# Shorter sums in the stick-breaking attention, and weighted sums two pairs behind the transposes

## The chip, the core and the metric

One NeuronCore of a Trainium2 chip runs the whole program in one launch. TensorE (PE, with its weight loads PEld), VectorE (DVE), ScalarE (ACT), GpSimd (POOL) and the DMA queue of SyncE (SP) run their own instruction lists side by side and meet only at semaphores. The metric is the device time of the launch in microseconds. Three runs of the kernel before gave 3422.81, 3422.94 and 3425.69 us; their median is 3422.94 us.

## The reference, cut to what matters

The model has two blocks on 512 tokens with 1024 features, all in float32. Two layers of the first block hold, between two feed-forward parts, a stick-breaking attention (4 heads) and a latent attention (8 heads). The second block has a sparse layer (attention over selected keys) and a dilated layer, and in each a memory attention over 256 memory tokens.

```
# stick-breaking attention, per block of 128 queries (4 heads)
z = q k^T * scale;  mask = key < query
log_not = where(mask, -softplus(z), 0)
after = reverse_cumsum(log_not, over keys) - log_not
w = where(mask, exp(log_sigmoid(z) + after), 0);  out = w v

# latent, sparse and memory attention: a softmax over keys
p = softmax(where(valid, s, NEG));  o = p v
```

The part of the change on the first attention is about `after`: for each key, the sum of `log_not` over all later keys. The part on the others is about the product `p v`.

## The kernel before, in words

Every weight is streamed in pieces of 128 x 1024 numbers. SP loads a piece, POOL splits it into a high and a low part (L524 writes the high, L526 the low part, both read and write SBUF), PE multiplies three times (high by high, low by high, high by low). Each engine's list is written by hand, in the order in which it is to run; a semaphore is waited for with `wait_ge` and raised by `then_inc`, and an instruction that waits holds all that stand behind it on its engine.

**Stick-breaking** (`stick_breaking_and_latent_heads` on PE and DVE, `stick_breaking` on ACT). The scores are kept with keys on the partitions. A unit is one block b of 128 keys of one head; a pair is the same block of two heads; `SB_PAIRS` is 2 head pairs c by 4 blocks, b = 3, 2, 1, 0. So u = 0..3 is c = 0 and u = 4..7 is c = 1. Per pair, PE writes z (L836, L838), ACT takes abs, exp and log (L1407 to L1411), DVE writes the softplus into `SBL` (L1728), PE adds the sums of the later keys into the bank of z (function `r`, L846), and ACT takes the exponential into `SBW` (L1417). In `r` the own block is multiplied by a triangle (`tri`) and every later block k by a matrix of ones (`onen`): block b = 3 takes one product, b = 0 takes four, of 512, 384, 256 and 128 columns. A float32 matmul is two records of the trace. PE runs `r` of pair u - 1 after the latent pieces and the z of pair u; `r` of the last pair stands alone at the end. DVE writes the softplus of pair u in step u, after the copies of the latent pieces.

**The other attentions** (`attend`, on PE, ACT and DVE) go over pairs of rows, a row being 128 queries of one head. In step j, PE makes the scores of pair j (L1010, L1016), transposes the probabilities of pair j - 3 (`turn_pair`, L1027), and multiplies the transposed ones of pair j - 4 by the values (`weigh`, L1045). DVE finds the row maximum of pair j (L1811) and scales the probabilities of pair j - 1 (L1820); ACT takes the exponential of pair j (L1452), then copies what PE transposed of pair j - 3 to SBUF (L1465, into `PRT`, which has 4 places for the sparse and memory attentions and 2 for the latent one), and at the end of a group of pairs the weighted sums (L1481); DVE then takes their low part (L1838). In the sparse attention DVE also runs the steps that select the keys (L1944, L1946) between the two. PE's transposes go to two banks in turn, so a group of up to 4 transposes waits until ACT has copied the group two before.

After the second memory attention DVE scales the probabilities of the dilated attention (L1894), PE transposes them (L967) and multiplies (L981). `keep_clock` (L620) issues matmuls whose results are not used.

Of the kernel before, what the change touches and what calls it, by code (L numbers as in the profile page):

```python
# [7 lines left out]
P = 128  # L8
D, S, DEPTH = 1024, 512, 2
KD = D // P  # L10
QB = S // P
# [106 lines left out]
def program(nc, A, trips):  # L118
# [3 lines left out]
    at = [-(-nc.sbuf_base // 32) * 32]  # L122
# [96 lines left out]
    def sem(name, start=0):  # L219
        credit[name] = start  # L220
        return ctx.enter_context(nc.semaphore(name))
# [22 lines left out]
    pj_done = sem("pj_done", 2)  # L244
    vt_ready, vt_done = sem("vt_ready"), sem("vt_done", 2)
    z_ready, zl_ready, zsp_ready, e_ready, w_ready = map(sem, ("z_ready", "zl_ready", "zsp_ready", "e_ready", "w_ready"))
    sbo_ready = sem("sbo_ready")
    cv_ready = sem("cv_ready")
    oh_ready, ol_ready = sem("oh_ready"), sem("ol_ready")
    ch_ready, cl_ready = sem("ch_ready"), sem("cl_ready")  # L250
# [122 lines left out]

    def ahead_of(which):

        return 2, 3

    BORDER_FILL = 3 * S
    START_FILL = {"dsa": 2 * S, "mem_dil": 2 * S}
# [206 lines left out]
    def _(pe):  # L586
# [237 lines left out]
        def stick_breaking_and_latent_heads():  # L824
# [15 lines left out]
            def r(i):  # L840
                c, b, x = SB_UNITS[i]
                pe.wait_ge(zsp_ready, n.full(zsp_ready))
                for k in range(b, QB):
                    o = sb_bank(i)[:, (k - b) * P:]
                    at = slice(sb_at(k), sb_at(k) + sb_w(k))
                    mm = pe.matmul(o, tri if k == b else onen, SBL[:, x, at], start=False, stop=k == QB - 1, skip_group_check=True)  # L846
                mm.then_inc(e_ready, 1)

            def pv(c):
# [136 lines left out]

        def attend(which, last_sums=None):
            pairs = pairs_of(which)
            ahead, late = ahead_of(which)
            pe.wait_ge(rot_done, n.now(rot_done))  # L990
            exp_base, out_base, turned_base = n.now(p_exp), n.now(ol_ready), n.now(pt_done)
            turns, weighed, group = 0, 0, 0
# [53 lines left out]
                                       skip_group_check=True)  # L1046
                mm.then_inc(pv_done, 1)

            for j in range(len(pairs) + late + 1):
                if j < len(pairs):  # L1050
                    scores(j)
                if last_sums is not None and j == 1:
                    last_sums()
                if which == "mem_dil" and j == 1:
                    dil_exchange()
                if which == "mem_dil" and j == 6:
                    pe.wait_ge(x_taken, n.full(x_taken))
                if 0 <= j - late < len(pairs):
                    turn_pair(j - late)
                if j - late - 1 >= 0:  # L1060
                    weigh(j - late - 1)
            n.full(p_exp, 2 * len(pairs))
            n.full(ol_ready, len(ends))

# [168 lines left out]
    def _(act):  # L1233
# [204 lines left out]

        def attend(which):
            pairs = pairs_of(which)  # L1440
            ahead, late = ahead_of(which)
            used_base, turns = n.now(pv_done), 0
            low_base = n.now(ol_ready)
            if which == "mla":
                n.full(ol_ready, 8)

            def exponentials(j):
                for x, row in enumerate(pairs[j]):
                    i, w = 2 * j + x, row_width(row)
                    if x == 0:  # L1450
                        act.wait_ge(nm_ready, n.full(nm_ready, 2))
                    act.activation(probs(which, i)[:, 0:w], score_bank(which, i)[:, 0:w], ACT.Exp, bias=stat[:, i % 8, 0:1],  # L1452
                                   accum_out=stat[:, i % 8, 1:2]).then_inc(p_exp, 1)

            def copy_turned(j):
                nonlocal turns
                slots = turned_slots(which)
                if j >= slots:
                    act.wait_ge(pv_done, used_base + j - slots + 1)
                if which == "mla" and j == 1:  # L1460
                    act.wait_ge(ol_ready, low_base + 4)
                for g, m in groups(pair_blocks(pairs[j])):
                    at = j % slots * 2 * S + g * P
                    act.wait_ge(pt_ready, n.full(pt_ready))
                    act.activation(PRT[which][:, at:at + m * P], PC[:, turns % 2, 0:m * P], ACT.Copy).then_inc(pt_done, 1)  # L1465
                    turns += 1

            for j in range(len(pairs) + late + 1):
                if which == "mem_dil" and j == 3:
                    dil_exchange()  # L1470
                if j < len(pairs):
                    exponentials(j)
                if which == "mla" and j == 1:
                    last_sums()
                if 0 <= j - late < len(pairs):
                    copy_turned(j - late)
                group = ended_group(which, j - late)
                if group is not None:
                    act.wait_ge(pv_done, used_base + j - late)
                    out, bank = heads_out(OH, PD[:, group % 2], which, group)  # L1480
                    act.activation(out, bank, ACT.Copy).then_inc(oh_ready, 1)  # L1481
            n.full(pv_done, len(pairs))
# [87 lines left out]
    def _(dve):  # L1570
# [152 lines left out]
        def stick_breaking_and_latent_heads():  # L1723
            def softplus(i):
                dve.wait_ge(zl_ready, n.full(zl_ready))
                if i == 2 * QB:
                    dve.wait_ge(e_ready, e_base + i)
                dve.scalar_tensor_tensor(out=SBL[:, i % 2, sb_part(i)], in0=sb_bank(i), scalar=0.0, in1=sb_exp(i),  # L1728
                                         op0=ALU.max, op1=ALU.add).then_inc(zsp_ready, 1)

            def latent_pieces(m):
                c = m // 2
                if m == 0:
                    dve.wait_ge(rc_ready, n.full(rc_ready, 2))
                dve.wait_ge(piece_used, n.full(piece_used))
                if m % 2 == 1:
                    dve.tensor_tensor(QM[:, c], PC[:, 0], RY[:], ALU.mult)
                    ins = dve.tensor_tensor(PROJ[:, c], PC[:, 1], YSS[:], ALU.mult)
                else:
                    if c < 2:  # L1740
                        dve.tensor_tensor(QM[:, 4 + c], PC[:, 1], RY[:], ALU.mult)
                    ins = dve.tensor_tensor(PROJ[:, C_SV + c], PC[:, 0], YSS[:], ALU.mult)
                ins.then_inc(mla_done, 1)
                n.full(mla_done)

            e_base = n.now(e_ready)
            for u in range(len(SB_PAIRS)):
                if u < 2:
                    softplus(2 * u)
                latent_pieces(u)  # L1750
                if u >= 2:
                    softplus(2 * u)
                softplus(2 * u + 1)
                if u in (0, 2):
                    turn([(QM[:, 4 + u // 2], P, tabM, C_PMLA)], PD[:, 1])
            n.full(e_ready, len(SB_UNITS))
# [45 lines left out]
        def attend(which, steps=None):  # L1802

            pairs = pairs_of(which)
            ahead, late = ahead_of(which)

            def peak(j):
                at = 2 * j % 8
# [10 lines left out]
                    p = probs(which, 2 * j + x)[:, 0:row_width(row)]  # L1819
                    dve.tensor_scalar(p, p, stat[:, at + x, 2:3], None, ALU.mult).then_inc(p_norm, 1)  # L1820

            for j in range(len(pairs) + late + 1):
                if which == "mem_dil" and j in (1, 2, 4):
                    (dil_spread, dil_gather, dil_factors)[(1, 2, 4).index(j)]()
                if j < len(pairs):
# [4 lines left out]
                    normalize(j - 1)  # L1830
                if which == "mla" and j in (1, 2):
                    last_sums(j)
                group = ended_group(which, j - late)
                if group is not None:
                    dve.wait_ge(oh_ready, n.full(oh_ready))
                    low, bank = heads_out(OL, PD[:, group % 2], which, group)
# [430 lines left out]
```

## Time and profile before

| what | value |
|---|---|
| median of 3 runs | 3422.94 us |
| profiled execution | 3417.32 us, span 3416.0 us |
| PE busy | 3322.6 us, 97% of the span |
| DVE, ACT, POOL busy | 1709.5, 717.5, 2415.8 us |
| mean granted PE clock | 0.994 of full speed |
| stick-breaking, both layers | 484 to 546 us and 1555 to 1617 us |
| sparse layer's attentions | 2302 to 2400 us |
| second memory attention | 2970 to 2997 us |

A row of the timeline gives the start of a group of like instructions in us from the span's start, and the time from the first's start to the last's end; the number in brackets is the engine's idle time just before and what ended it. Matmuls overlap, so what a group costs is read from its start to the start of what follows.

### The profile page before, as it was taken

How to read it: one execution, taken by the hardware profiler on the slowest of the kernel's cores; microseconds unless marked ns; L12 is line 12 of the kernel's file. 1: busy time of each engine (PE TensorE's matmuls, PEld its weight loads, DVE VectorE, ACT ScalarE, POOL GpSimd, SP SyncE). 2: the span in 40 equal slices, each digit the busy share in tenths (PEclk: the TensorE clock that was granted, in tenths of full speed). 3: DMA queues.
4: the chain of work that ended last, by engine and by line, in shares of the span. 5: the costliest groups of instructions: out<-in, count | busy, mean ns of one | idle time of the engine just before them, and what ended most of it. 6: DMA issues, size and time to landing. Idle time of an engine off the chain costs nothing.

```text
span 3416.0 us, 42138 instructions
## 1 busy us (share of the span) xinstructions
PE 3322.6 (97%) x15386; PEld 2628.0 (77%) x15389; DVE 1709.5 (50%) x1889; ACT 717.5 (21%) x1447; POOL 2415.8 (71%) x1115
## 2 busy tenths in 40 slices
PE   8999999999999999999999999998999999999998
PEld 7888775788887888776678887674788877778887
DVE  5454444554657546154464574688554234454521
ACT  3111125311114111123421113316211101331100
POOL 8888762588886888865278887660688786548875
PEclk9999999999999999999999999999999999999999
DMA  3223220222332223322022233220222222112232
GB/s 132 98 94 106 92 87 32 87 86 98 108 129 71 91 98 102 117 70 79 32 87 98 98 110 109 93 87 1 80 93 98 99 103 100 65 56 96 95 104 93
DMA packets 84367, 305.15 MB, mean 89 GB/s; under 512 B 9360, under 2 KB 9616, under 8 KB 83984
## 3 DMA queue, kind: packets, MB, share of 16 engines
q1 hardware_dynamic: 80928, 292.59, 25.3%
q10 hardware_dynamic: 3312, 10.86, 0.9%
q8 instruction: 81, 1.33, 0.2%
q14 instruction: 46, 0.38, 0.0%
HBM read 299.22 MB, written 4.19 MB: 89 GB/s over the span
## 4 chain that ended last, share of the span: by engine, by line
PE 88%; DVE 6%; ACT 3%; issue 3%; DMA 0%; DVEq 0%; ACTq 0%
PE psC L600 12%; PE psC L602 12%; PE psC L601 12%; PE psA L600 8%; PE psA L602 8%; PE psA L601 8%; PE psB L600 5%; PE psB L601 5%; PE psB L602 5%; PE psC L1072 1%; PE psC L1073 1%; PE psC L1074 1%; DVE stat L1811 1%; DVE X L1600 1%; DVE HL L1584 1%
## 5 line engine op out<-in xcount | busy, mean ns | idle before, releaser
L524 POOL TENSOR_TENSOR WH<-raw,scalars 128x1024 fp32r<-128x1024 f32 (+1 forms) x554 | 1049.5, 1894 | 931.9 <-DMA raw<-in_w 864.0
L526 POOL TENSOR_TENSOR WL<-raw,WH 128x1024 fp32r<-128x1024 f32 (+1 forms) x554 | 1363.7, 2462 | 43.4
L600 PE MATMUL psA<-HH,WH 128*128 128x512 f32 x1136 | 454.3, 400 | 2.2 <-DVE PROJ L1903 2.2
L602 PE MATMUL psA<-HL,WH 128*128 128x512 f32 x1136 | 442.9, 390 | 0.0
L601 PE MATMUL psA<-HH,WL 128*128 128x512 f32 x1136 | 442.7, 390 | 0.0
L600 PE MATMUL psC<-HIDH,WH 128*128 128x512 f32 x1056 | 416.1, 394 | 0.0
L602 PE MATMUL psC<-HIDL,WH 128*128 128x512 f32 x1056 | 414.0, 392 | 0.0
L601 PE MATMUL psC<-HIDH,WL 128*128 128x512 f32 x1056 | 409.8, 388 | 0.0
L1673 DVE TENSOR_TENSOR HIDL<-Y,HIDH 128x512 f32 (+1 forms) x132 | 258.9, 1961 | 125.7 <-ACT HIDH L1314 125.7
L600 PE MATMUL psC<-HH,WH 128*128 128x512 f32 x704 | 275.9, 392 | 0.0
L601 PE MATMUL psC<-HH,WL 128*128 128x512 f32 x704 | 274.3, 390 | 0.0
L602 PE MATMUL psC<-HL,WH 128*128 128x512 f32 x704 | 274.3, 390 | 0.0
L600 PE MATMUL psB<-HH,WH 128*128 128x512 f32 x696 | 272.1, 391 | 0.0
L601 PE MATMUL psB<-HH,WL 128*128 128x512 f32 x696 | 271.1, 390 | 0.0
L602 PE MATMUL psB<-HL,WH 128*128 128x512 f32 x696 | 271.0, 389 | 0.0
L1671 DVE TENSOR_TENSOR Y<-Y 128x512 f32<-128x512 f32 x132 | 251.1, 1902 | 21.3 <-DVE Y L1668 10.5
L600 PEld LDWEIGHTS psA<-HH,WH 128*128 128x128 f32 x1136 | 213.3, 188 | 57.0 <-issue 10.2
L601 PEld LDWEIGHTS psA<-HH,WL 128*128 128x128 f32 x1136 | 213.2, 188 | 49.4 <-issue 5.5
L1314 ACT ACTIVATE HIDH<-Y 128x512 f32 x132 | 83.5, 632 | 788.9 <-DVE Y L1671 788.9
L602 PEld LDWEIGHTS psA<-HL,WH 128*128 128x128 f32 x1136 | 213.3, 188 | 45.3
L602 PEld LDWEIGHTS psC<-HIDL,WH 128*128 128x128 f32 x1056 | 198.2, 188 | 46.4
L601 PEld LDWEIGHTS psC<-HIDH,WL 128*128 128x128 f32 x1056 | 198.2, 188 | 44.4
(370 smaller groups left out, 4798.9 us busy)
## 6 DMA issues: line engine op xcount, KB each, us to landing
raw<-in_w SPq DMA_DIRECT2D x554, 512.0 KB, 3.3
X<-in_x ACTq DMA_DIRECT2D x4, 512.0 KB, 9.0
NRAW<-in_mem ACTq DMA_DIRECT2D x2, 1024.0 KB, 5.3
out<-Y SPq DMA_DIRECT2D x8, 256.0 KB, 2.1
POSI<-in_pos ACTq DMA_DIRECT2D x4, 256.0 KB, 2.7
PRAW<-in_p ACTq DMA_DIRECT2D x2, 512.0 KB, 3.6
table_F<-newF ACTq DMA_DIRECT2D x2, 512.0 KB, 3.4
table_I<-newI ACTq DMA_DIRECT2D x2, 512.0 KB, 4.4
```

The lines of the kernel that those rows point to most:

```text
L524: pool.tensor_tensor(WH[j][:, 0:w], raw[j][:, 0:w], zero[:, 0:1].broadcast_to([P, w]), ALU.subtract).then_inc(w_hi, 1)
L526: pool.tensor_tensor(WL[j][:, 0:w], raw[j][:, 0:w], WH[j][:, 0:w], ALU.subtract).then_inc(w_split, 1)
L600: pe.matmul(out, WH[slot][:, w], hi[:, t], start=start and t == 0, stop=False)
L601: pe.matmul(out, WL[slot][:, w], hi[:, t], start=False, stop=False)
L602: mm = pe.matmul(out, WH[slot][:, w], lo[:, t], start=False, stop=stop and t == tiles - 1)
L1072: pe.matmul(out, WH[slot][:, w], OH[which][:, t], start=i == 0, stop=False)
L1073: pe.matmul(out, WL[slot][:, w], OH[which][:, t], start=False, stop=False)
L1074: mm = pe.matmul(out, WH[slot][:, w], OL[which][:, t], start=False, stop=t == order[-1])
L1314: act.activation(HIDH[:, bass.ds(2 * i + j, 1)].rearrange("p a n -> p (a n)"), US[:, j], ACT.Copy).then_inc(hidh_ready, 1)
L1584: dve.scalar_tensor_tensor(out=HL[:, k], in0=X[:, k], scalar=gain(k), in1=HH[:, k], op0=ALU.mult, op1=ALU.subtract).then_inc(hl_ready, 1)
L1671: dve.tensor_tensor(US[:, j], US[:, j], GS[:, j], ALU.mult).then_inc(hf_ready, 1)
L1673: dve.tensor_tensor(HIDL[:, at].rearrange("p a n -> p (a n)"), US[:, j], HIDH[:, at].rearrange("p a n -> p (a n)"), ALU.subtract).then_inc ...
```

## The change

In the stick-breaking attention, `r` now multiplies only the own block and the next one. For blocks b = 1 and b = 0 the next block's `SBL` is first made to hold the sum of all later blocks: DVE adds block b + 2 onto block b + 1 in place (`add_later_block`, both heads in one instruction), and raises a new semaphore, `later_ready`, for which PE waits at the first head of these pairs. DVE issues the add for pair u - 1 at the start of its step u, and one more step is added for the last pair. In `attend`, the sparse and memory attentions weigh pair j - 5 in step j instead of pair j - 4; the latent attention stays as it was.

```diff
@@ PE @@
             def r(i):
                 c, b, x = SB_UNITS[i]
                 pe.wait_ge(zsp_ready, n.full(zsp_ready))
-                for k in range(b, QB):
+                if x == 0 and b < QB - 2:
+                    pe.wait_ge(later_ready, n.full(later_ready))
+                for k in range(b, min(b + 2, QB)):
                     o = sb_bank(i)[:, (k - b) * P:]
                     at = slice(sb_at(k), sb_at(k) + sb_w(k))
...
-            for j in range(len(pairs) + late + 1):
+            for j in range(len(pairs) + late + weighed_late):
...
-                if j - late - 1 >= 0:
-                    weigh(j - late - 1)
+                if j - late - weighed_late >= 0:
+                    weigh(j - late - weighed_late)
@@ all engines @@
-        return 2, 3
+        return 2, 3, 1 if which == "mla" else 2
@@ ACT @@
-                group = ended_group(which, j - late)
+                finished = j - late - weighed_late + 1
+                group = ended_group(which, finished)
                 if group is not None:
-                    act.wait_ge(pv_done, used_base + j - late)
+                    act.wait_ge(pv_done, used_base + finished)
@@ DVE @@
+            def add_later_block(u):
+
+                b = SB_PAIRS[u][1]
+                if b >= QB - 2:
+                    return
+                own = slice(sb_at(b + 1) + P, sb_at(b + 1) + sb_w(b + 1))
+                later = slice(sb_at(b + 2), sb_at(b + 2) + sb_w(b + 2))
+                dve.wait_ge(e_ready, e_base + 2 * u)
+                dve.tensor_tensor(SBL[:, :, own], SBL[:, :, own], SBL[:, :, later], ALU.add).then_inc(later_ready, 1)
+
             e_base = n.now(e_ready)
-            for u in range(len(SB_PAIRS)):
+            for u in range(len(SB_PAIRS) + 1):
+                if u > 0:
+                    add_later_block(u - 1)
+                if u == len(SB_PAIRS):
+                    break
                 if u < 2:
                     softplus(2 * u)
...
-                group = ended_group(which, j - late)
+                group = ended_group(which, j - late - weighed_late + 1)
```

On DVE, at the end of the stick-breaking attention, before (`SBL` is the softplus, the last two writes are the two heads of the last pair; the first rows behind are the latent attention's):

```order
L1738 TENSOR_TENSOR PROJ<-psC,YSS 128x512
L1725 REGISTER_ALU
L1728 SCALAR_TENSOR_TENSOR SBL<-psA,SBE_130 128x512
L1725 REGISTER_ALU
L1728 SCALAR_TENSOR_TENSOR SBL<-psA,SBE_130 128x512
L1811 TENSOR_REDUCE stat<-psB 128x2
```

and now:

```order
L1742 TENSOR_TENSOR PROJ<-psC,YSS 128x512
L1729 REGISTER_ALU
L1732 SCALAR_TENSOR_TENSOR SBL<-psA,SBE_130 128x512
L1729 REGISTER_ALU
L1732 SCALAR_TENSOR_TENSOR SBL<-psA,SBE_130 128x512
L1758 TENSOR_TENSOR SBL<-SBL 128x2x256
L1829 TENSOR_REDUCE stat<-psB 128x2
```

The add for the last pair stands behind both softplus writes of that pair.

On PE, at the same place, before (the sums of the last two pairs, first b = 1, then b = 0; two heads each):

```order
L846 MATMUL psB<-SBL,cf 128x128
L846 MATMUL psA<-SBL,cf 128x512
L846 MATMUL psA<-SBL,cf 128x384
L846 MATMUL psA<-SBL,cf 128x256
L846 MATMUL psA<-SBL,cf 128x128
L846 MATMUL psA<-SBL,cf 128x512
L846 MATMUL psA<-SBL,cf 128x384
L846 MATMUL psA<-SBL,cf 128x256
L846 MATMUL psA<-SBL,cf 128x128
L1010 MATMUL psB<-PROJ,QM 128x128 x4
```

and now:

```order
L848 MATMUL psB<-SBL,cf 128x256
L848 MATMUL psA<-SBL,cf 128x512
L848 MATMUL psA<-SBL,cf 128x384
L848 MATMUL psA<-SBL,cf 128x512
L848 MATMUL psA<-SBL,cf 128x384
L1013 MATMUL psB<-PROJ,QM 128x128 x4
```

The last pair has four products instead of eight, and those of 256 and 128 columns are gone.

On PE, at the end of the sparse attention, before (L1027 transposes, L1045 weighted sums; then the out-projection):

```order
L1027 MATMUL psC<-cf,PR 128x128 x8
L1045 MATMUL psD<-PRTb,VT 64x128 x8
L1027 MATMUL psC<-cf,PR 128x128 x8
L1045 MATMUL psD<-PRTb,VT 64x128 x16
L107 UNCONDITIONAL_BRANCH
```

and now:

```order
L1030 MATMUL psC<-cf,PR 128x128 x8
L1048 MATMUL psD<-PRTb,VT 64x128 x8
L1030 MATMUL psC<-cf,PR 128x128 x8
L1048 MATMUL psD<-PRTb,VT 64x128 x24
L107 UNCONDITIONAL_BRANCH
```

Three pairs' weighted sums follow the last transposes instead of two.

## Rows read from the trace of the kernel before

**Rows 1.** The page, parts 1 and 4: engines' busy time; chain by engine.
```profile
PE 3322.6 (97%) x15386; PEld 2628.0 (77%) x15389; DVE 1709.5 (50%) x1889; ACT 717.5 (21%) x1447; POOL 2415.8 (71%) x1115
...
PE 88%; DVE 6%; ACT 3%; issue 3%; DMA 0%; DVEq 0%; ACTq 0%
```

**Rows 2.** Waits of PE, whole span: total us, times, longest us.
```profile
PE psD L1045 <- ACT PRTb L1465: 10.7, 14, 1.3
...
PE psC L1027 <- ACT PRTb L1465: 4.2, 7, 1.1
```

**Rows 3.** Timeline of PE, stick-breaking: start, length, engine, line, operation, count [idle before].
```profile
517.05 0.49 PE L836 MATMUL psB<-PROJ 64*128 64x128 f32 x4 [0.48 <-ACT SBW L1417]
...
517.60 4.53 PE L846 MATMUL psA<-SBL,cf 128*128 128x512 f32 x16
521.97 0.60 PE L889 MATMUL psD<-cf,PROJ 128*128 128x128 f32 x4
...
541.49 4.58 PE L846 MATMUL psA<-SBL,cf 128*128 128x512 f32 x16
546.00 0.91 PE L1010 MATMUL psB<-PROJ,QM 64*128 64x128 f32 x8
...
1616.54 0.91 PE L1010 MATMUL psB<-PROJ,QM 64*128 64x128 f32 x8
```

**Rows 4.** Timeline of DVE, stick-breaking in both layers.
```profile
494.83 0.68 DVE L1793 TENSOR_TENSOR QM<-QM,tabM 128x512 f32<-128x512 f32 x1
...
509.31 1.73 DVE L1793 TENSOR_TENSOR QM<-QM,tabM 128x512 f32<-128x512 f32 x1
...
516.27 0.69 DVE L1728 SCALAR_TENSOR_TENSOR SBL<-psA,SBE 128x512 f32<-128x512 f32 x1 [1.12 <-ACT SBE L1411]
...
542.55 0.69 DVE L1728 SCALAR_TENSOR_TENSOR SBL<-psA,SBE 128x512 f32<-128x512 f32 x1 [1.12 <-ACT SBE L1411]
...
1613.09 0.69 DVE L1728 SCALAR_TENSOR_TENSOR SBL<-psA,SBE 128x512 f32<-128x512 f32 x1 [1.12 <-ACT SBE L1411]
```

**Rows 5.** Timeline of POOL, the same stretches.
```profile
508.91 1.58 POOL L526 TENSOR_TENSOR WL<-raw,WH 128x640 fp32r<-128x640 f32 x1
...
516.08 1.55 POOL L526 TENSOR_TENSOR WL<-raw,WH 128x640 fp32r<-128x640 f32 x1
...
542.75 1.90 POOL L524 TENSOR_TENSOR WH<-raw,scalars 128x1024 fp32r<-128x1024 f32 x1 [3.69 <-DMA raw<-in_w]
...
1613.56 2.35 POOL L526 TENSOR_TENSOR WL<-raw,WH 128x1024 fp32r<-128x1024 f32 x1
```

**Rows 6.** Timeline of PE: three places where it waited about 2 us or more.
```profile
558.85 0.44 PE L1045 MATMUL psD<-PRTa,VT 128*64 128x128 f32 x4 [1.96 <-ACT PRTa L1465]
...
1629.39 0.49 PE L1045 MATMUL psD<-PRTa,VT 128*64 128x128 f32 x4 [1.96 <-ACT PRTa L1465]
...
3035.03 0.50 PE L1072 MATMUL psC<-OHb,WH 128*128 128x512 f32 x1 [2.57 <-DVE X L1648]
```

**Rows 7.** Stretches: us, busy of PE, PEld, DVE, ACT, POOL (counts), PE clock, DMA.
```profile
558.85:566.00 7.15, 7.15 (x60) 4.38 (x62) 3.59 (x10) 3.80 (x14) 0.00 (x0) 1.00 0.01 3
1629.80:1637.20 7.40, 7.40 (x34) 3.85 (x32) 1.54 (x5) 2.42 (x9) 0.00 (x0) 0.55 0.01 3
3035.90:3039.30 3.40, 3.40 (x10) 2.62 (x9) 3.40 (x4) 1.60 (x3) 3.32 (x2) 0.51 0.02 5
2325.00:2369.00 44.00, 35.02 (x296) 20.86 (x292) 39.56 (x109) 28.72 (x98) 0.00 (x0) 1.00 0.00 1
```

**Rows 8.** Timeline of PE, the end of the sparse attention.
```profile
2398.14 1.97 PE L1045 MATMUL psD<-PRTb,VT 128*64 128x128 f32 x32
```

**Rows 9.** Waits of PE in the last memory attention (2970 to 2998).
```profile
PE psD L1045 <- ACT PRTb L1465: 2.0, 4, 0.7
```

**Rows 10.** Timeline of DVE there.
```profile
2987.09 0.69 DVE L1811 TENSOR_REDUCE stat<-psA 128x2 f32<-128x512 f32 x1 [0.95 <-PE psA L1010]
```

More of the change, by code:

```diff
@@ L246, in program @@
     z_ready, zl_ready, zsp_ready, e_ready, w_ready = map(sem, ("z_ready", "zl_ready", "zsp_ready", "e_ready", "w_ready"))
-    sbo_ready = sem("sbo_ready")
+    sbo_ready, later_ready = sem("sbo_ready"), sem("later_ready")
     cv_ready = sem("cv_ready")
@@ L842, in r @@
                 pe.wait_ge(zsp_ready, n.full(zsp_ready))
-                for k in range(b, QB):
+                if x == 0 and b < QB - 2:
+                    pe.wait_ge(later_ready, n.full(later_ready))
+                for k in range(b, min(b + 2, QB)):
                     o = sb_bank(i)[:, (k - b) * P:]
                     at = slice(sb_at(k), sb_at(k) + sb_w(k))
-                    mm = pe.matmul(o, tri if k == b else onen, SBL[:, x, at], start=False, stop=k == QB - 1, skip_group_check=True)
+                    mm = pe.matmul(o, tri if k == b else onen, SBL[:, x, at], start=False, stop=k == min(b + 1, QB - 1),
+                                   skip_group_check=True)
                 mm.then_inc(e_ready, 1)
@@ L988, in attend @@
             pairs = pairs_of(which)
-            ahead, late = ahead_of(which)
+            ahead, late, weighed_late = ahead_of(which)
             pe.wait_ge(rot_done, n.now(rot_done))
@@ L1440, in attend @@
             pairs = pairs_of(which)
-            ahead, late = ahead_of(which)
+            ahead, late, weighed_late = ahead_of(which)
             used_base, turns = n.now(pv_done), 0
@@ L1466, in copy_turned @@
                     turns += 1
-            for j in range(len(pairs) + late + 1):
+            for j in range(len(pairs) + late + weighed_late):
                 if which == "mem_dil" and j == 3:
@@ L1804, in attend @@
             pairs = pairs_of(which)
-            ahead, late = ahead_of(which)
+            ahead, late, weighed_late = ahead_of(which)
             def peak(j):
@@ L1820, in normalize @@
                     dve.tensor_scalar(p, p, stat[:, at + x, 2:3], None, ALU.mult).then_inc(p_norm, 1)
-            for j in range(len(pairs) + late + 1):
+            for j in range(len(pairs) + late + weighed_late):
                 if which == "mem_dil" and j in (1, 2, 4):
```

## The prediction

> **What bounds the kernel now.** I read the page first. PE is busy for 3322.6 of 3416.0 us and holds 88% of the chain that ended last, so only time on PE, or a wait of PE, can move the end [rows 1]. Then PE's waits over the whole span: its longest by total are those of the weighted sums for ACT's copies of the transposed probabilities, 10.7 us in 14 places, and behind them those of the transposes for the same copies, 4.2 us in 7 [rows 2]. The change takes work from PE in the stick-breaking attention and aims at the first of these waits in the others. So I read both places in order of time: in the stick-breaking attention PE, DVE and POOL side by side [rows 3 to 5], in the others what DVE and PE do while the other waits [rows 7 to 10].
>
> **The stick-breaking sums: the work that goes.** The sums of the pair c = 0, b = 0 start at 517.60 and the next work on PE starts at 521.97, so they cost 4.37 us; the 0.60 us that the printed length adds is overlap of the last matmul [rows 3]. Of 512 + 384 + 256 + 128 columns the change leaves 512 + 384, so 30% goes: 1.31 us, and 3.06 us is left. A pair with b = 1 loses 128 columns, by the same rate 0.44 us. Each layer has two pairs of either kind: 3.5 us a layer, 7.0 us in all. If all of it stayed, that would be the gain. I now follow each of the four.
>
> (1) c = 0, b = 1. The next wait of PE is at 517.05, 0.48 us for ACT's exponentials (L1417) [rows 3]. ACT is then behind on a chain that began with z, not with these sums. The 0.44 us makes this wait longer: gain 0.
>
> (2) c = 0, b = 0. The sums now also wait for the add. On DVE the add stands behind the second head's softplus, which ran from 516.27 to 516.96 [rows 4]. The trace has no such add; the nearest row is L1793, on 512 elements too, with both inputs in SBUF: 0.68 us at 494.83, but 1.73 us at 509.31 [rows 4]. There POOL's L526 ran from 508.91 to 510.49 [rows 5], and L1793 ended at 511.04, 0.55 us after it: it did not run slowly, it stood until POOL's instruction was over. The softplus at 516.27 and at 542.55, with one input in PSUM, kept its 0.69 us beside POOL's work [rows 4, 5]. For the add, POOL's L526 runs from 516.08 to 517.63 [rows 5], so it ends near 518.2, PE starts near 518.3 instead of 517.60 and ends at 521.36 instead of 521.97: gain 0.6 us, in both layers 1.2 (the second layer repeats these rows).
>
> In these rows only L526 is seen to hold DVE up; I take the same for L524, which also reads and writes SBUF, and it is in the way in (4).
>
> The Trainium skill, SBUF — State Buffer, section "Who interferes with whom", says that a DVE instruction with two SBUF inputs contends with any GpSimd instruction that reads SBUF, and that whichever comes second stands for the whole of the first. By that rule L524 blocks as L526 does, and the sum is as below. By the rows alone, if L524 did not, the first layer's add would end near 543.85 and the sum would be 1.4 us smaller.
>
> (3) c = 1, b = 1. Its add finds room before its sums start; the sums are 0.44 us shorter, and the time flows into the wait of (4): gain 0.
>
> (4) c = 1, b = 0, the last pair, is where the change costs. Before, PE started the first head's sums at 541.49, as soon as that head's softplus was there, while ACT and DVE still made the second head's; that one ended at 543.24 [rows 3, 4]. Now the first head's sums wait for the add, and the add stands behind the second head's softplus. POOL's L524 holds SBUF from 542.75 to 544.65 [rows 5], so the add ends near 545.25 and the sums run from 545.3 to 548.36. Before, the next work started at 546.00 [rows 3]: 2.35 us later. In the second layer softplus ends at 1613.78 and POOL's L526 runs from 1613.56 to 1615.91, so the add ends near 1616.5, the sums near 1619.6, against 1616.54 [rows 3 to 5]: 3.07 us later. Behind PE's wait stand the scores of the latent attention, which DVE and ACT need next; nothing hides it. Bounds: if the add finds the ports free it ends 0.6 us after the softplus and the sums 0.9 us later than before; a full L526 (2.35 us) in its way makes that 3.2 us.
>
> Sum without the clock, both layers: -1.2 + 2.35 + 3.07 = +4.2 us.
>
> **PE's clock behind the stall.** In (4) PE stands from about 541.05 (541.49 less the 0.44 us) to 545.3, some 4.3 us, and about 5 us in the second layer. After a wait of 2.57 us [rows 6] the granted clock was 0.51, the lower level of 1.2 GHz, from 3035.9 to 3039.3; after one of 1.96 us at 1629.39 it was 0.55 for 7.4 us; after another of 1.96 us at 558.85 it stayed at 1.00 (2.4 GHz) [rows 6, 7]. Longer stalls are not in the trace of a busy stretch, so I bound: 0 (no fall), 3.4 x 0.49 = 1.7 us, 7.4 x 0.45 = 3.3 us a layer. I take 1.7, the value beside the longest wait of the three: +3.4 us for both layers.
>
> By the Trainium skill, TensorE: Matmul & The Clock Gate, section "What's actually happening", the clock is low by default and falls back after idleness; by it every stall of this length would lower it, as my sum has it. By the row at 558.85 it need not: then the sum would be 3.4 us smaller.
>
> **The weighted sums, sparse attention.** Taking the sum one pair later removes the need for the newest copy. But the 10.7 - 2.0 = 8.7 us that PE waits so in this layer [rows 2, 9] would be gained only if DVE and ACT could go faster. From 2325 to 2369 DVE is busy 39.56 of 44 us [rows 7]; its gaps are the waits for ACT's copy of a finished group, which comes in the same order as before. DVE's row maximum and scaling set the pace, and PE will wait elsewhere: at the transposes or at the scores. After 2369 the waits of PE already stand at the transposes (the second line of [rows 2]), which the change does not move. At the end, three pairs' sums follow the last transposes instead of two; in the row of the last two, 32 records take 1.97 us less 0.07 of overlap, so one pair is 0.95 us, and it comes where nothing waits any more [rows 8]. Against it stands that DVE may see a few scores earlier, as in [rows 10]. I take a third of the 0.95, +0.3 us, between -2 (two such waits of DVE gone) and +1.
>
> **The second memory attention.** Here it helps. PE's waits for the copies are 2.0 us in 4 [rows 9], and one of them held the scores for which DVE then waited 0.95 us [rows 10]; and the last scaling no longer stands behind a group's low part on DVE. The scaling of the dilated attention follows on DVE, and PE waits for that. I take the 0.95 and half of the other 1.0: -1.4 us, between -2 and 0. The first memory attention is paced by DVE's selection steps: 0.
>
> **Sum.** 4.2 + 3.4 + 0.3 - 1.4 = +6.5 us. On the profiled execution's 3417.32 us that is 3423.8; the median of the runs shown lies 5.62 us above that execution, so for a median I predict 3422.94 + 6.5 = 3429.4 us. Two medians of this kernel can tell about 0.2%, 6.85 us, from no change: a faster result lies below 3416.1, a slower above 3429.8.
>
> **The rivals.**
>
> *The clock falls for longer.* If each stall costs what 1629.8 to 1637.2 did, 3.3 us instead of 1.7, the sum is +9.7: 3432.6 us, slower. For it: these stalls are about twice the longest in [rows 6]. Against it: a part of the slow time passes while PE stands. It decides from 0.4 us above my sum on, so it is close.
>
> *The adds find their place.* POOL's phase depends on when its DMAs land (its L524 at 542.75 had waited 3.69 us for one [rows 5]). If the adds run at once and the clock stays, (4) costs 0.9 us a layer: -1.2 + 1.8 + 0.3 - 1.4 = -0.5, 3422.4 us, no change.
>
> *The waits really go.* If PE's running ahead lets the whole loop of the sparse and memory attentions turn faster, the 10.7 us of [rows 2] go and no other wait takes their place; with the stick-breaking part at -1.2 + 1.8 = +0.6 the sum is -10.1: 3412.8 us, faster. For it: DVE did wait for PE's scores [rows 10]. Against it: DVE's 39.56 of 44 us.
>
> **How the numbers follow.** Forecast 0.48, with a range of its own from 3426 to 3433 (an add that waits for 0 to 2.35 us, one layer's clock more or less); longer slow clock 0.25; adds find their place 0.15; waits go 0.12. Above 3429.8 I count 0.2 of the forecast and 0.22 of the longer clock: slower 0.42. Faster is 0.12. The rest, 0.46, is within 0.2%. The range that leaves out 2 in 10 goes from 3419 (no stall, the upper gain in the memory attention, -2 in the sparse one) to 3436 (both stalls at 3.2 us and 3.3 us of clock, +1 in the sparse one, nothing in the memory one, is +12.8).
>
> **What would show it.** In the profile after: the last pair's sums on PE start about 4 us after the pair before them has ended, with a wait for DVE's add in front; adds that lie beside POOL last 1.2 to 2.4 us, others 0.4 to 0.7; the clock is near 0.5 in a stretch behind one or both stalls. In the sparse attention the waits at the weighted sums are gone, those at the transposes and scores have grown, and its end is within 1 us of before relative to its start; the second memory attention is 1 to 2 us shorter. I am wrong if PE starts the last sums right after the pair before, or if the sparse attention is over 2 us shorter.

## The result and the profile after

The changed kernel takes 3435.72 us in the median of 8 runs (3432.49 to 3441.1), the kernel before 3422.88 us in 8 runs beside them: 12.84 us slower, ratio 1.0036, 95% interval 1.0027 to 1.0046. I had predicted 3429.4 us, with 3419 to 3436 as the range. The sign and the main place are as predicted; the loss of 6.5 us that I worked out is half of what it is, and the time lies only 0.3 us inside the upper end of the range. The profiled execution took 3436.3 us with a span of 3435.0.

First the page and the waits of PE over the whole span (total us, times, longest us), which answer to [rows 1, 2].

```profile
PE 3325.3 (97%) x15341; PEld 2623.8 (76%) x15341; DVE 1720.8 (50%) x1897; ACT 717.2 (21%) x1447; POOL 2412.6 (70%) x1115
...
PE 86%; DVE 7%; issue 3%; ACT 3%; DMA 0%; DVEq 0%; ACTq 0%
```
```profile
PE psA L848 <- DVE SBL L1758: 11.3, 4, 5.1
...
PE psC L1030 <- ACT PRTb L1468: 7.3, 7, 2.5
...
PE psA L1013 <- ACT PR L1455: 4.4, 6, 1.9
PE psB L1013 <- ACT PR L1455: 4.2, 8, 1.1
```

PE has 45 records less but is busy 2.7 us longer: matmuls went, and others ran at the lower clock. The wait of the weighted sums for the copies, 10.7 us in [rows 2], is gone from the list. In its place the transposes wait 7.3 us for the copies instead of 4.2, the scores wait for the exponentials, and on top stands a new wait of 11.3 us, four times, that of the stick-breaking sums for DVE's add (L1758).

Now the last pair of the stick-breaking attention, which answers to [rows 3 to 5]: PE, DVE and POOL in the first layer.

```profile
517.26 0.49 PE L836 MATMUL psB<-PROJ 64*128 64x128 f32 x4 [0.93 <-ACT SBW L1420]
...
518.58 3.25 PE L848 MATMUL psA<-SBL,cf 128*128 128x512 f32 x8 [0.60 <-DVE SBL L1758]
521.66 0.60 PE L892 MATMUL psD<-cf,PROJ 128*128 128x128 f32 x4
...
538.34 2.37 PE L848 MATMUL psB<-SBL,cf 128*128 128x384 f32 x8
545.68 4.91 PE L848 MATMUL psA<-SBL,cf 128*128 128x512 f32 x8 [4.97 <-DVE SBL L1758]
550.52 0.91 PE L1013 MATMUL psB<-PROJ,QM 64*128 64x128 f32 x8
...
563.37 0.70 PE L1048 MATMUL psD<-PRTa,VT 128*64 128x128 f32 x4 [1.97 <-ACT PRTa L1468]
```
```profile
517.09 1.34 DVE L1758 TENSOR_TENSOR SBL<-SBL 128x512 f32<-128x512 f32 x1
...
542.24 0.69 DVE L1732 SCALAR_TENSOR_TENSOR SBL<-psA,SBE 128x512 f32<-128x512 f32 x1 [1.12 <-ACT SBE L1414]
542.85 2.68 DVE L1758 TENSOR_TENSOR SBL<-SBL 128x512 f32<-128x512 f32 x1
```
```profile
540.67 1.90 POOL L524 TENSOR_TENSOR WH<-raw,scalars 128x1024 fp32r<-128x1024 f32 x1 [1.88 <-DMA raw<-in_w]
542.64 2.34 POOL L526 TENSOR_TENSOR WL<-raw,WH 128x1024 fp32r<-128x1024 f32 x1
```

The add begins when softplus is over, stands until POOL's L526 ends at 544.98, and ends 0.55 us later. PE has waited 4.97 us by then, and the sums take 4.91 us where the first half's, the same eight matmuls, took 3.25. The second layer is the same, with more of the sums at the slow clock:

```profile
1625.12 6.20 PE L848 MATMUL psA<-SBL,cf 128*128 128x512 f32 x8 [5.06 <-DVE SBL L1758]
1631.24 0.91 PE L1013 MATMUL psB<-PROJ,QM 64*128 64x128 f32 x8
```

The stretches behind these waits (us, busy of PE, PEld, DVE, ACT, POOL with counts, granted clock, DMA), which answer to [rows 7]:

```profile
545.70:550.50 4.80, 4.80 (x8) 2.15 (x8) 0.00 (x0) 0.60 (x1) 0.00 (x0) 0.65 0.02 3
1625.20:1631.20 6.00, 6.00 (x8) 2.41 (x8) 0.00 (x0) 0.60 (x1) 0.00 (x0) 0.51 0.01 3
563.40:571.00 7.60, 7.60 (x38) 4.17 (x39) 1.92 (x6) 2.80 (x11) 0.00 (x0) 0.60 0.00 1
```

The sums ran mostly (0.65) or nearly wholly (0.51) at the lower level of 1.2 GHz. DVE and POOL did nothing in either stretch. The third line is the stretch behind the wait of 1.97 us at 563.37: its like had the clock at 1.00 in the kernel before [rows 7].

The end of the sparse attention, which answers to [rows 8], on PE and DVE; the last fence has two lines of the kernel before, the last row maximum on DVE and, on PE, the group that waits in the first fence:

```profile
2404.27 1.09 PE L1048 MATMUL psD<-PRTb,VT 128*64 128x128 f32 x16
2407.84 1.06 PE L1030 MATMUL psC<-cf,PR 128*128 128x128 f32 x8 [2.47 <-ACT PRTb L1468]
2408.83 1.56 PE L1048 MATMUL psD<-PRTb,VT 128*64 128x128 f32 x16
2410.33 1.97 PE L1030 MATMUL psC<-cf,PR 128*128 128x128 f32 x8
...
2414.50 2.84 PE L1048 MATMUL psD<-PRTb,VT 128*64 128x128 f32 x48
2417.27 0.50 PE L1075 MATMUL psC<-OHa,WH 128*128 128x512 f32 x1
```
```profile
2404.03 0.56 DVE L1856 TENSOR_TENSOR OLa<-psD,OHa 128x384 fp32r<-128x384 f32 x1 [1.88 <-ACT OHa L1485]
2404.51 1.22 DVE L1829 TENSOR_REDUCE stat<-psB 128x2 f32<-128x1024 f32 x1
```
```profile
2389.71 1.23 DVE L1811 TENSOR_REDUCE stat<-psB 128x2 f32<-128x1024 f32 x1 [0.35 <-PE psB L1016]
...
2393.06 1.06 PE L1027 MATMUL psC<-cf,PR 128*128 128x128 f32 x8 [0.49 <-ACT PRTb L1465]
```

DVE takes the low part of a finished group (`OLa`), for which it waits 1.88 us on ACT's copy, and only then the very last row maximum; before, that row maximum waited 0.35 us for its scores and for nothing else. The last exponentials and the copies that stand behind them on ACT are late, the transposes wait 2.47 us instead of 0.49, the clock falls (a transposing group takes 1.97 us, another 1.06), and three weighted sums follow.

Against the kernel before, by the start of the same instruction in both profiled executions: from the first scores of the stick-breaking attention to the first scores of the latent one the first layer lost 4.31 us and the second 5.71; the sparse attention lost 3.95; the second memory attention gained 1.87. Together that is 12.1 us. The two profiled spans differ by 19.0 us; the other 6.9 us lie in places that the change does not touch (the last section shows one of them).

### The profile page after: what moved, and what is told of

It reads as the page before. It is cut to its first block, busy times and chain, and to the rows that moved or that the text cites. A ratio compares the mean times of both kernels' runs of the same rounds, so it can differ in the third digit from the quotient of the medians.

```text
span 3435.0 us, 42061 instructions
## 1 busy us (share of the span) xinstructions
PE 3325.3 (97%) x15341; PEld 2623.8 (76%) x15341; DVE 1720.8 (50%) x1897; ACT 717.2 (21%) x1447; POOL 2412.6 (70%) x1115
## 4 chain that ended last, share of the span: by engine, by line
PE 86%; DVE 7%; issue 3%; ACT 3%; DMA 0%; DVEq 0%; ACTq 0%
PE psC L600 12%; PE psC L602 12%; PE psC L601 12%; PE psA L600 8%; PE psA L602 8%; PE psA L601 8%; PE psB L600 5%; PE psB L601 5%; PE psB L602 5%; PE psC L1075 1%; PE psC L1077 1%; PE psC L1076 1%; DVE HL L1588 1%; DVE X L1604 1%; DVE stat L1829 1%
## 5 line engine op out<-in xcount | busy, mean ns | idle before, releaser
L524 POOL TENSOR_TENSOR WH<-raw,scalars 128x1024 fp32r<-128x1024 f32 (+1 forms) x554 | 1047.5, 1891 | 954.1 <-DMA raw<-in_w 885.3
L526 POOL TENSOR_TENSOR WL<-raw,WH 128x1024 fp32r<-128x1024 f32 (+1 forms) x554 | 1362.2, 2459 | 43.4
```

Source lines behind the costliest of these rows:

```text
L524: pool.tensor_tensor(WH[j][:, 0:w], raw[j][:, 0:w], zero[:, 0:1].broadcast_to([P, w]), ALU.subtract).then_inc(w_hi, 1)
L526: pool.tensor_tensor(WL[j][:, 0:w], raw[j][:, 0:w], WH[j][:, 0:w], ALU.subtract).then_inc(w_split, 1)
```

## The experiments

The times are medians of 5 to 12 runs; the kernel before ran beside each and had 3422.2 to 3422.9 us. Differences are against it, with the 95% interval of the ratio.

**The parts of the change.** Each of the three alone.

```diff
 a_only:  return 2, 3, 1                                     # new sums; weighed late nowhere
 b_dsa:   return 2, 3, 2 if which == "dsa" else 1            # old sums
 b_mem:   return 2, 3, 2 if which == "mem_dil" else 1        # old sums
```


> Only the stick-breaking part of the change; all weighted sums one pair behind the transposes as in the kernel before. Theory 1 (the loss is made by the last pair's sums, which wait for an add that stands behind the second head's softplus and a POOL instruction, and by the clock that falls there): slower by 10 to 13 us, because in the changed kernel's profile the start of the sparse attention is 13.3 us later than before, of which up to 2.7 us is a clock fall that may or may not repeat. Theory 2 (the loss belongs to the weighed-late part and the late start of the sparse attention is an accident of one execution): within 3 us of before. My prediction on record has +7.6 us for this part.

> The stick-breaking sums as in the kernel before; only the sparse attention has its weighted sums two pairs behind. Theory 1 (the group's low part on DVE now falls in front of the last row maximum, so the last transposes wait about 2 us longer and three weighted sums follow them): slower by 3 to 5 us, and the same 2.2 to 2.5 us waits at the last transposes are in the profile. Theory 2 (that end was only late because the clock fell there by chance): slower by 0 to 1.5 us. My prediction on record has +0.3 us for this part.

> The stick-breaking sums as in the kernel before; only the second memory attention has its weighted sums two pairs behind. Theory 1 (two waits go, at DVE's row maxima and at PE's last sums, 1.87 us in the changed kernel's profile, and the stretch that follows gains 1.4 us because no wait there pulls the clock down): faster by 1.5 to 3.3 us. Theory 2 (what is gained comes back as a longer wait at the exchange that the dilated attention depends on): within 0.5 us. My prediction on record has -1.4 us.

Measured: stick-breaking part 3435.53 us, +12.7 (1.0026 to 1.0054); sparse attention 3425.62 us, +2.8 (1.0001 to 1.0019); second memory attention 3421.05 us, -1.8 (0.9984 to 1.0002). The three add up to +13.6, the whole change has +12.8: within the intervals the parts do not touch each other. The loss is in the stick-breaking sums. The interval of the memory attention includes no change, and in the profile of that kernel the stretch is 0.60 us shorter. The sparse part lost a little less than theory 1 had; alone it shows the late end again, in a profile where nothing before it was changed:

```profile
2398.79 1.83 PE L1027 MATMUL psC<-cf,PR 128*128 128x128 f32 x8 [2.47 <-ACT PRTb L1465]
```

**The place of the add.** For b = 0 the later sums go to a buffer of their own, so that the add need not wait until the pair before has used its operand, and runs one pair earlier. The edit in short:

```diff
-dve.wait_ge(e_ready, e_base + 2 * u)
-dve.tensor_tensor(SBL[:, :, own], SBL[:, :, own], SBL[:, :, later], ALU.add)   # b = 0
+dve.wait_ge(zsp_ready, sp_base + 2 * u)        # softplus of the pair before
+dve.tensor_tensor(LATER[:], SBL[:, :, own], SBL[:, :, later], ALU.add)
...
+parts = [tri x SBL block 0, onen x SBL block 1 [0:P], onen x LATER]            # PE, b = 0
```


> The stick-breaking part with the add of the last block pair's later sums written to a buffer of its own, so that it need not wait until the pair before has read its operand: it runs one pair earlier, before the softplus of the pair that uses it. PE multiplies the same 896 columns for that pair as in the changed kernel, in three matmuls instead of two; the other pairs as in the changed kernel; weighted sums as before. Theory 1 (the loss is the place of the add, not the add): the last pair's first sums start at their softplus again, about 541.5 us, and end 1.2 us sooner than in the kernel before; with 0.6 us of the first half that is 1.8 to 2.5 us a layer, faster by 3.5 to 5 us in all. Theory 2 (the added DVE work holds softplus up by as much as PE saves): within 1 us of before. Theory 3 (POOL's hold on SBUF is the loss wherever the add stands): slower by 2 us or more.

Measured: 3418.96 us, -3.9 (0.9974 to 0.9992). From the stick-breaking scores to the latent ones the two layers gain 2.30 and 2.25 us against before. PE in the first layer, and the add on DVE:

```profile
539.57 1.35 PE L851 MATMUL psA<-SBL,cf 128*128 128x512 f32 x4 [0.51 <-DVE SBL L1734]
...
542.52 0.60 PE L851 MATMUL psA<-LATER,cf 128*128 128x256 f32 x2
543.05 0.91 PE L1015 MATMUL psB<-PROJ,QM 64*128 64x128 f32 x8
```
```profile
511.47 0.69 DVE L1766 TENSOR_TENSOR LATER<-SBL 128x512 f32<-128x512 f32 x1
...
534.98 2.74 DVE L1766 TENSOR_TENSOR LATER<-SBL 128x512 f32<-128x512 f32 x1
```

The first line is the add of the layer's first half, with POOL idle. The add of the last pair stood for POOL again (2.74 us), but here PE did not wait for it. So the idea of summing the later blocks on DVE is worth 3.9 us; where the add stood cost 16.6.

The second way to the same end keeps the add in its pair and only moves it on DVE's queue, between the two heads' softplus.

```diff
 softplus(2 * u)
+if SB_PAIRS[u][1] == 0: add_later_block(u)
 softplus(2 * u + 1)
```


> As the stick-breaking part alone (that ran at +12.7 us), but for b = 0 the add stands between the two heads' softplus instead of behind the second. Theory 1 (its place is the loss): POOL's instruction that runs from 540.8 to 542.7 us still holds the add, PE starts the last sums near 542.9 us instead of 545.8 and waits 2.2 us instead of 5.0, the second head's softplus follows at 542.8 and its sums end near 545.9 us, about what the kernel before has (546.0): +1 to +3 us against the kernel before, where a fall of the clock behind the 2.2 us wait would make the upper end. Theory 2 (POOL's hold is the loss, wherever the add stands): +8 us or more.

Measured: 3422.72 us, +0.5 (0.9993 to 1.0013): theory 1 holds, the time a little under it. PE's wait is 2.54 us in the first layer, where the sums behind it take 3.25 us, and 2.46 us in the second, where they take 4.81 us. The add and POOL's instruction beside it, in the first layer:

```profile
539.60 2.06 DVE L1758 TENSOR_TENSOR SBL<-SBL 128x512 f32<-128x512 f32 x1
```
```profile
539.21 1.89 POOL L524 TENSOR_TENSOR WH<-raw,scalars 128x1024 fp32r<-128x1024 f32 x1 [1.81 <-DMA raw<-in_w]
```

The add ends at 541.66, 0.56 us after L524.

**POOL's hold and the clock, each taken away.** One kernel reads the add's second operand from PSUM: it takes the maximum with the pair's own scores, and so leaves out the sum over the later blocks. The other fills the wait with matmuls whose results are not used. The edits in short:

```diff
 a_nolock: -..., SBL[:, :, later], ALU.add)   +..., (PB, PA)[u % 2][:, :, 0:sb_w(b + 2)], ALU.max)
 a_clock:  +if u == len(SB_PAIRS): pe.wait_ge(mla_done, ...); keep_clock(PC[:, 0], 5 * S)
```


> As the stick-breaking part alone (+12.7 us), but the add's second operand comes from PSUM (the pair's own scores, same size, as a maximum), so that it has one input in SBUF only. It leaves out the sum over later blocks, nothing else. Theory 1 (an instruction of DVE with two inputs in SBUF stands until POOL's is over): the add takes 0.7 us instead of 2.75, the last sums start 2 us earlier in both layers and PE's wait is 3.0 instead of 5.0 us: faster than the stick-breaking part alone by 4.1 us, by up to 9 us if the clock then stays. Theory 2 (the add is as long by itself): no difference.

> As the stick-breaking part alone (+12.7 us), but with five matmuls of 512 columns on a spare bank (4.3 us of work at the upper clock, no effect on the result) in front of the last pair's sums, in PE's wait of 5.0 us. Theory 1 (of the last sums' 4.85 and 6.2 us in the two layers 1.8 and 3.1 us are the clock that fell in the wait): these sums take 3.1 us again; faster than the stick-breaking part alone by 3 to 5 us. Theory 2 (the sums are slow for another reason, such as contention for SBUF): no difference, or slower by what the matmuls outlast the wait.

Measured: 3428.05 us, +5.8 (1.0004 to 1.0025), and 3428.22 us, +6.0 (1.0008 to 1.0028): 6.9 and 6.7 us less than the +12.7 of the stick-breaking part alone, each against the kernel before beside it. DVE and POOL in the kernel with the PSUM operand:

```profile
541.86 0.68 DVE L1758 TENSOR_TENSOR SBL<-SBL,psA 128x512 f32<-128x512 f32 x1
```
```profile
541.63 2.35 POOL L526 TENSOR_TENSOR WL<-raw,WH 128x1024 fp32r<-128x1024 f32 x1
```

Beside the same POOL instruction the add now takes 0.68 us instead of 2.68. PE's wait is 2.96 us in both layers; behind it the sums took 3.25 us in one layer and 4.70 in the other:

```profile
1616.44 4.70 PE L848 MATMUL psA<-SBL,cf 128*128 128x512 f32 x8 [2.96 <-DVE SBL L1758]
```

The sums of the two layers with the stick-breaking part alone, then those of the first layer in the kernel with the filled wait (3.25 us there in both layers):

```profile
545.84 4.85 PE L848 MATMUL psA<-SBL,cf 128*128 128x512 f32 x8 [5.04 <-DVE SBL L1758]
...
1625.11 6.22 PE L848 MATMUL psA<-SBL,cf 128*128 128x512 f32 x8 [5.09 <-DVE SBL L1758]
```
```profile
542.79 4.46 PE L620 MATMUL psC<-cf 128*128 128x512 f32 x10
548.03 3.25 PE L848 MATMUL psA<-SBL,cf 128*128 128x512 f32 x8 [0.79 <-DVE SBL L1761]
```

So POOL held the add, and the clock slowed the sums. The Trainium skill, SBUF — State Buffer, section "Who interferes with whom", says that a DVE instruction with at most one input in SBUF, outside its two-port modes, does not contend with GpSimd; the 0.68 us agree. The two gains overlap, since the shorter wait also kept the clock in one layer. The filled wait gained 6.7 us where I expected 3 to 5: the sums are 1.6 + 3.0 = 4.6 us shorter, and what the other 2.1 us are these runs do not show. Nor do the single profiles account for the medians: from the stick-breaking scores to the latent ones the two layers together lose 1.5 us against before with the PSUM operand, where the median has 5.8, and 8.7 us with the filled wait, where the median has 6.0.

**The sparse attention.** DVE's wait for ACT's copy of a finished group, in the range from 2300 to 2400 of the kernel before: total us, times, longest.

```profile
DVE OLa L1838 <- ACT OHa L1481: 9.2, 8, 2.2
```

The low part was put one pair later, first with the weighted sums two pairs behind, then with them one behind as before.

```diff
-group = ended_group(which, j - late - weighed_late + 1)
+group = ended_group(which, j - late - weighed_late)          # DVE, "dsa"; the last group as before
```


> The sparse attention alone with its weighted sums two pairs behind (+2.8 us by its own run), with one more step: DVE takes the low part of a finished group one pair later, so that at the end it stands behind the last row maximum and not in front of it, and DVE finds ACT's copy done. Theory 1 (the low part in front of the last row maximum makes the last transposes late): the wait of 2.5 us at the last transposes goes, and the run is 2 to 4 us faster than with the low part where it was: -1 to +1 us against the kernel before. Theory 1b (the waits of DVE for these copies, some 1.9 us for each of the eight groups, also set the pace of the loop): faster than the kernel before by 2 to 8 us. Theory 2 (the end is late because three pairs' sums follow and the clock falls there): no difference from the run before it, +2 to +4 us.

> The kernel before, with weighted sums one pair behind everywhere, and only DVE's low part of a finished group of the sparse attention one pair later. Theory 1 (DVE's wait for ACT's copy of a finished group sets the pace of the loop, 13.6 us in 9 waits, and to give PE the sums a pair later only helps when that wait is loosened too): faster than before by 2 to 4 us, less than the 4.7 us of both steps together, since PE still waits at the weighted sums for the newest copies. Theory 2 (the low part's place is all there is to it): faster by 4 to 6 us, as with both. Theory 3 (both steps are needed): within 1 us of before.

Measured: 3417.58 us, -4.7 (0.9977 to 0.9994), and 3416.45 us, -5.8 (0.9973 to 0.9992). Both are faster, and the simpler one not less: theory 2 of the second. By the profiles the loop of the sparse layer's attentions, from its first scores to the out-projection, is 5.19 and 5.24 us shorter than before, so that the two kernels do not differ there. The same part of the loop (from the first scores over tokens to the first scores of the widest rows) in three kernels, before, with the weighted sums two behind, and with the low part later alone; columns as above:

```profile
2325.12:2369.76 44.64, 35.66 (x304) 21.45 (x302) 40.16 (x112) 29.32 (x101) 0.00 (x0) 1.00 0.00 1
```
```profile
2329.18:2374.43 45.25, 37.14 (x301) 22.31 (x299) 40.61 (x114) 29.00 (x100) 0.00 (x0) 0.96 0.00 1
```
```profile
2328.20:2368.81 40.61, 35.48 (x304) 21.44 (x302) 39.44 (x111) 28.80 (x99) 0.00 (x0) 1.00 0.01 1
```

DVE does about the same 40 us of work in each. In the third it is busy for 39.44 of 40.61 us: its waits for the copy of a finished group, 3.4 us in this part before, are gone, while PE still waits for the newest copies (4.3 us in 8). To take the weighted sums two behind did not shorten this part; PE's waits moved from the weighted sums to the scores.

The same for the second memory attention:

```diff
+group = ended_group(which, j - late - weighed_late)          # DVE, "mem_dil", weighed two behind
```


> The second memory attention alone with its weighted sums two pairs behind (-1.8 us by its own run), and with DVE's low part of a finished group one pair later as well. Theory 1 (as in the sparse attention, DVE's wait for ACT's copy holds the loop): faster than before by 3 to 5 us. Theory 2 (with two groups in eight pairs there is too little of it): no difference from the run without it, -1 to -3 us.

Measured: 3421.75 us, -0.5 (0.9989 to 1.0007), against -1.8 without it: no gain from the low part there.

**Together.**

```diff
 best:   a_early + weighed two behind in "dsa" and "mem_dil" + low part later in "dsa"
 best1:  the same, "dsa" one behind
```


> All that the runs so far speak for: the stick-breaking sums with the later sums added early into a buffer of their own (-3.9 us alone), the weighted sums of the sparse attention two pairs behind with DVE's low part one pair later (-4.7 us alone), those of the second memory attention two pairs behind (-1.8 us alone). Theory 1 (the three act in different stretches and add up): faster than before by 9 to 11.5 us. Theory 2 (what is gained early is lost again at the next wait for a transfer or a slower clock): faster by 3 to 7 us.

> As the fastest kernel so far (12.1 us under before), but with the weighted sums of the sparse attention one pair behind again; DVE's low part stays one pair later. Theory 1 (the second pair of distance is worth nothing in the sparse attention once the low part has moved): within 2 us of that kernel, some 10.5 to 13 us under before. Theory 2 (it is worth what the waits at the weighted sums still show, 5.5 us in the kernel with the low part alone moved): 6 to 8 us under before.

Measured: 3410.22 us, -12.1 (0.9955 to 0.9979), and 3413.45 us, -9.2 (0.9958 to 0.9982). The first is above the sum of its parts (-10.4), within its interval, and faster than both kernels of this study: 24.9 us under the changed one, each against before. Whether the second pair of distance in the sparse attention is worth anything is not settled: -9.2 lies between the two theories and the intervals overlap, and the pair of runs above (-4.7 with it, -5.8 without) points the other way.

## Why the prediction was half right

The time lies inside the range, at its very end, and outside the forecast's own 3426 to 3433. The end of the range, +12.8, was made of both stalls and both slow clocks at their worst, +1 in the sparse attention and nothing in the memory one. That is not how the 12.84 us came about, so that they lie inside is in part luck.

**The work that goes.** The sum holds, but one reading is wrong: the printed 4.53 us are 0.16 us more than the 4.37 from start to start, not 0.60. Nothing rests on it.

**Terms 1 and 3, gain 0.** Right: in the first layer PE's wait for the exponentials is 0.93 us (517.26) instead of 0.48, which is where the 0.44 us of term 1 went. What the first half saved is still there at the last pair (softplus at 542.24 instead of 542.55, 0.3 us), and it goes into the wait.

**Term 2, gain 0.6 us.** Measured 0.5 in either layer: in the first PE is 0.21 us late before these sums and 0.31 us early after them (521.66 against 521.97). The add was held as I had read from L1793, 1.34 us beside L526.

**Term 4, the last pair.** The mechanism is what happened; this term, with its clock, was sized too small. I had the sums of the first layer start at 545.3, they start at 545.68 in a kernel that is 0.31 us early there: 0.7 us more, since POOL's next transfer had landed earlier and nearly a whole L526 stood in the way instead of the rest of an L524. That L524 holds DVE too, which I had only assumed, is shown by the kernel with the add between the heads. My clock term was 1.7 us a layer; the sums were 1.66 and 2.95 us longer than at the upper clock (4.91 and 6.20 less 3.25), so 4.6 instead of 3.4. The filled wait, behind which the same sums took 3.25 us, shows that this is the clock and not contention. The predicted step between the two scores is 3.45 and 4.17 us (term 4 with its clock, less term 2); measured 4.31 and 5.71. So in this profile the stick-breaking part lost 10.0 us, not 7.6. By its median alone it lost 12.7. The 2.7 us between the two I can't assign. The profiled execution of before was itself 5.6 us under the median of its runs, and differences of this size come and go with the clock in places that the change does not touch (last section).

**The sparse attention, +0.3 us.** This step failed: +2.8 by its own runs, 3.95 in the profile. I had seen that DVE's gaps are the waits for ACT's copy of a finished group, and rightly said that they stay. But I counted the end as a part of one weighted sum more, a third of 0.95 us, and did not follow where the last low part comes in DVE's order: in front of the last row maximum. That makes the last transposes 2 us later (2.47 us of wait in place of 0.49), and the clock falls behind it. With the low part one pair later the loss is gone. The rival "the waits really go" was wrong in its means: PE's running ahead did not speed the loop. It was right that a gain lay there, about half of the one it named, but in DVE's waits, which I had put down as part of DVE's own pace. Without them the part of the loop read above takes 40.6 us instead of 44.6.

**The second memory attention, -1.4 us.** Measured -1.8, with an interval that includes no change, 1.87 in the profile of the change and 0.60 in that of the part alone: not contradicted, and not shown either.

**The rivals.** "The clock falls for longer" (3432.6 us) came nearest: of it the second layer is true. "The adds find their place" is what two of the experiments built: +0.5 and -3.9 us against my -0.5.

## What to carry to other kernels

When work moves from the engine that bounds a kernel to another, look at what is queued in front of it there and who waits behind it: the same sum on DVE cost 12.7 us behind both softplus, 0.5 us between them, and gained 3.9 one pair earlier with a buffer of its own. In a loop over pairs, an instruction that waits for another engine's copy should stand where that copy is long done; in the sparse attention one pair later gave 5.8 us, in the second memory attention nothing that shows. The wait that was longest in PE's list gave nothing that these runs settle when it was removed. Follow the last iteration of a changed loop instruction by instruction; an average over the loop doesn't show it.

## What was unexpected of the hardware

The clock does not answer alike to a wait of the same length. The wait of 1.96 or 1.97 us at the first weighted sums of the first layer's latent attention is in all fourteen profiled executions, with the same work before and behind it. In nine the attention then took 1.6 to 4.7 us longer than in the other five, which agree within 0.01 us (56.1 us from its first scores to the out-projection). One of either kind, the kernel with the memory attention's part alone and the fastest kernel; the granted clock is the last figure but two:

```profile
558.30:566.00 7.70, 7.70 (x36) 4.09 (x36) 1.92 (x6) 2.79 (x11) 0.00 (x0) 0.53 0.01 3
```
```profile
557.30:564.50 7.20, 7.20 (x60) 4.36 (x62) 3.56 (x10) 3.84 (x15) 0.00 (x0) 1.00 0.01 3
```

In 7.7 us the one did 36 matmuls, in 7.2 us the other 60. The kernel before was one of the five when it was profiled. Waits of 2.5 and 3.0 us in front of the stick-breaking sums lowered the clock in one layer of each kernel and not in the other, those of about 5 us all four times. The Trainium skill, TensorE: Matmul & The Clock Gate, section "What's actually happening", says that the point at which the clock rises after the start of a kernel varies from run to run of the same kernel. It speaks of the start and not of a wait further on; here each kernel was profiled once, so that no run shows this wait in one kernel twice. What the runs show of one kernel is the mean granted clock: of the kernel before, 0.995 in the run of 3416.86 us and 0.992 in the one of 3430.11 us. A single profile against another can so mislead by some 5 us; medians average over it, within the intervals given.

DVE and POOL meet not only at semaphores. An add of 512 elements with two inputs in SBUF ended 0.55 us after the POOL instruction in whose time it began, in each of these rows: 544.98 and 545.53 in the changed kernel, 541.10 and 541.66 with the add between the heads. Where POOL was still it took 0.69 us (the early add of the first half), so nearly all of it came after POOL, and its price is what is left of POOL's instruction plus 0.55 us. An add of 256 elements in the changed kernel ended at 536.55, 0.27 us after POOL's L524.
